# Stage edges of a fused two-layer decoder step, and the order of key groups in its sample attention

## The chip, the cores and the metric

The kernel runs on one core of a Trainium2 chip. The metric is the device time in microseconds (us), the median of three runs. One more execution was taken with the hardware profiler; all rows and line numbers come from it.

## The reference

One inference step of a hybrid trunk, here with 2 layers, for a prompt of 1024 tokens and 8 sample sequences of 8 tokens, 1088 tokens of width 1024, in fp32:

- every layer makes 6 modulation vectors per sequence from a conditioning vector (`ada = c @ w_ada + b`), modulates x with two of them, and projects it to the inputs of three head groups: gated linear attention (GLA, 4 heads), a gated linear recurrence (LRU, 256 wide) and multi-head latent attention (MLA, 8 heads, latent width 128, rotary part 32);
- the prompt tokens attend causally to themselves; each sample sequence attends to 8192 cached tokens, in a cache of pages of latent rows and rotary key rows, and to its own new tokens;
- `x <- LN(alpha * x + gate * (mix @ w_out))`, then a modulated SwiGLU feed-forward part (FFN) with hidden width 2816 and the same closing norm.

The outputs are the rows of x, the final states, and the new latent and rotary rows.

## The kernel before

`build` holds the whole program. It runs `stage_start`, and then for each layer `stage_in` (input projections, convolution, LRU), `stage_gla`, `stage_mla_prompt`, `stage_mla_sample` and `stage_out_ffn`. `run` (L200) starts a stage, and behind it clears the stage's semaphores and has all engines meet at a barrier, so nothing of a stage starts before the last instruction of the one before. Within a stage the order of the work is written out by hand, engine by engine, and semaphores tie the engines together. Loads are issued by SP (SyncE), page gathers by POOL (GpSimd).

**Three passes.** fp32 products of weights are made as three products of rounded halves: `three_passes` (L441) multiplies hi by hi (L444), then lo by hi or hi by lo (L445, L446, by operand). ACT rounds a tile to its "hi" and DVE subtracts to get the "lo"; both must be there before PE starts on the tile.

**`stage_start` (L2929).** Loads x and the first adaLN weights (WADA, 4 pieces j of 2 MB, 16 column blocks), normalizes the rows of x, and turns them back to feature-major form: 24 groups `back(g)` (L3032) of up to three 128x128 turns, kept by DVE and ACT by turns. Between them PE makes `ada(j)` (L478, 16 products each); ACT copies the rows out of PSUM (L2997). Behind all of it PE turns the 16 rows into vectors (L3045), DVE adds the bias (L450), scales (L456), and ACT (L411) and DVE (L413) modulate x into h. DVE makes the page indices there too.

**`stage_in` (L575).** Loads `w_in_B` (8 rows k), ACT rounds h and w_in_B for each k (L846, L848), DVE makes the remainders (L975), PE multiplies (first one at L444). Scans for the LRU stand at its end.

**`stage_gla` (L1061).** Works through 9 blocks of tokens in steps: `cumulate(p)` (L1122 to L1124) makes the cumulated log decay, DVE the scaled queries and keys (L1305 to L1327, the last four small products per block put the queries of each head in their own rows), `attend`, `output`. The other weights of adaLN come through here too: slabs of 1 MB (`ada_load`), for each a `pair` of products (L478, 16 of them), 24 pairs in layer 0 and 16 in layer 1, `ADA_PER_STEP` says how many in each step. POOL multiplies the LRU output by its gate at the stage's start (L1109).

**`stage_mla_prompt` (L1437).** 64 items of attention (4 pairs of heads hp, 16 items each). PE scores an item (L1597, L1599), DVE takes the negative maximum (L1775), ACT exponentiates (L1728), DVE inverts the sums, ACT scales the probabilities (L1712), PE turns them (L1609), DVE or ACT copy them (L1788), PE multiplies by the values (L1621). The head projections of the next pair (q L1569, keys L1572, latent query L1576) are put between the items: `pj_at` has ten of them at ten steps in a row, from step 5 of each 16. ACT reads them out (L1696, L1698, L1700) behind its scale of the step. POOL adds rotary parts (L1522).

**`stage_mla_sample` (L1843).** 32 pieces s, 4 for each sequence, of 2048 cached tokens. A piece has four groups of key latents and one of rotary keys (KG = 5), each of four 128x128 turns (L1910) into one of three PSUM banks, from where ACT copies three (L2002), DVE one, and ACT and DVE split the rotary group into hi (L2017) and lo (L2083). `scores` waits for all five, then makes six rotary products (L1923) and eight halves of the latent ones (L1928). Then the maximum (L2065), the exponential (L2034), `turn` (L1940), the copy of the turned probabilities (L2008, half each), `values` (L1951) and `accumulate` (L2075). PE's order for a piece is scores(s), keys(s+1) with the rotary group last, values(s-1), turn(s). Before piece 0 stands the attention to the new tokens (L1958, L1962), with a copy into the running output. Behind the last piece come a chain of small operations that joins the halves (L1976 to L2110), a product that folds them (L1985) and the value projection (L1993, DVE copies at L2116). POOL gathers the pages (L1881) and rotary rows (L1887) from the stage's start, 5 pages deep.

**`stage_out_ffn` (L2240).** SP loads w_out in 8 rows k; ACT rounds the mixed heads (L2567) and w_out (L2572), DVE makes the remainders (L2861, L2863), PE multiplies from L444. In the last layer eight products that spread the gains of the norm (L2426) stand before it. Then the FFN with its seven-product scheme, and the closing norm.

## Time and profile before

| what | us |
|---|---|
| median of 3 runs (3478.95 to 3488.6) | 3480.62 |
| profiled execution, its own time | 3485.3 |
| its span, first to last instruction | 3483.5 |
| mean granted TensorE clock, as a share of 2.4 GHz | 0.966 |
| start | 0 to 53.9 |
| layer 0: input | 53.9 to 238.2 |
| layer 0: GLA | 238.2 to 343.6 |
| layer 0: prompt attention | 343.6 to 565.9 |
| layer 0: sample attention | 565.9 to 856.1 |
| layer 0: output and FFN | 856.1 to 1766.2 |
| layer 1: input, GLA, prompt, sample, output and FFN begin at | 1766.2, 1951.4, 2049.1, 2275.3, 2565.9 |

In the rows below, PE is TensorE's matmul side and PEld its weight loads, which overlap it; DVE is VectorE, ACT ScalarE, POOL GpSimd. A line of a timeline has start, duration, engine, line of the kernel, operation, output<-inputs, and x with the count of neighbouring instructions taken together; in square brackets the idle time of the engine before it and what ended that. PEclk is the granted clock as a share of 2.4 GHz: 0.5 is the lower level, 1.2 GHz.

### The profile page before, as it was taken

How to read it: one execution, taken by the hardware profiler on the slowest of the kernel's cores; microseconds unless marked ns; L12 is line 12 of the kernel's file. 1: busy time of each engine (PE TensorE's matmuls, PEld its weight loads, DVE VectorE, ACT ScalarE, POOL GpSimd, SP SyncE). 2: the span in 40 equal slices, each digit the busy share in tenths (PEclk: the TensorE clock that was granted, in tenths of full speed). 3: DMA queues.
4: the chain of work that ended last, by engine and by line, in shares of the span. 5: the costliest groups of instructions: out<-in, count | busy, mean ns of one | idle time of the engine just before them, and what ended most of it. 6: DMA issues, size and time to landing. Idle time of an engine off the chain costs nothing. (4 is left out here: it accounts for less than half of the span.)

```text
span 3483.5 us, 61376 instructions
## 1 busy us (share of the span) xinstructions
PE 3255.1 (93%) x23676; PEld 2738.1 (79%) x23676; DVE 2326.5 (67%) x4390; ACT 1587.2 (46%) x3159; POOL 202.9 (6%) x254
## 2 busy tenths in 40 slices
PE   6988898998999999999989889989989999999997
PEld 4875566776998998999978655667769899899997
DVE  5254665444488889888844456644446888888878
ACT  5343554444255454444344445634433554544432
POOL 0020111110000000000001111011100000000000
PEclk9998999998999999999989889999989999999998
DMA  7026102443033332222121340044421333322231
GB/s 272 27 93 230 66 1 105 164 157 106 16 106 96 95 101 80 90 87 86 52 109 31 137 142 1 1 163 165 158 49 52 94 98 96 94 87 83 91 106 57
DMA packets 158149, 334.72 MB, mean 96 GB/s; under 512 B 18556, under 2 KB 85406, under 8 KB 146471
## 3 DMA queue, kind: packets, MB, share of 16 engines
q1 hardware_dynamic: 146342, 246.91, 22.2%
q0 software_dynamic: 11520, 83.89, 6.8%
q8 instruction: 193, 3.16, 0.4%
q14 instruction: 94, 0.76, 0.1%
HBM read 315.32 MB, written 15.43 MB: 95 GB/s over the span
## 5 line engine op out<-in xcount | busy, mean ns | idle before, releaser
L2494 ACT CAST w_ffn_hi<-w_ffn 128x512 fp32r<-128x512 f32 x616 | 371.3, 618 | 259.4 <-DVE w_ffn L2676 128.0
L445 PE MATMUL psum<-h_lo,w_ffn_hi 128*128 128x256 f32 (+1 forms) x1408 | 406.6, 289 | 0.0
L2688 DVE TENSOR_TENSOR w_ffn_lo<-w_ffn,w_ffn_hi 128x1024 fp32r<-128x1024 f32 (+1 forms) x366 | 383.0, 1047 | 11.8 <-ACT w_ffn_hi L2494 11.7
L444 PE MATMUL psum<-h_forms_hi,w_ffn_hi 128*128 128x288 f32 x1232 | 364.1, 296 | 3.4 <-DVE w_ffn_lo L2688 3.4
L446 PE MATMUL psum<-h_forms_hi,w_ffn_lo 128*128 128x288 f32 x1232 | 363.7, 295 | 0.0
L444 PE MATMUL psum<-h_hi,w_ffn_hi 128*128 128x256 f32 x1232 | 348.6, 283 | 10.9 <-DVE w_ffn_lo L2688 9.1
L444 PE MATMUL psum<-ffn_act_hi,w_down_hi 128*128 128x288 f32 (+1 forms) x992 | 332.3, 335 | 21.1 <-DVE w_down_lo L2694 6.5
L446 PE MATMUL psum<-h_hi,w_ffn_lo 128*128 128x256 f32 x1232 | 346.8, 281 | 0.0
L446 PE MATMUL psum<-ffn_act_hi,w_down_lo 128*128 128x288 f32 (+1 forms) x992 | 326.6, 329 | 0.0
L445 PE MATMUL psum<-ffn_act_lo,w_down_hi 128*128 128x288 f32 (+1 forms) x992 | 325.9, 328 | 0.0
L430 DVE SCALAR_TENSOR_TENSOR xT<-psum,adaT,xT 128x512 f32<-128x512 f32 (+2 forms) x320 | 191.1, 609 | 130.4 <-PE psum L446 127.0
L445 PEld LDWEIGHTS psum<-h_lo,w_ffn_hi 128*128 128x128 f32 x1408 | 265.0, 188 | 0.6
L444 PEld LDWEIGHTS psum<-h_hi,w_ffn_hi 128*128 128x128 f32 x1232 | 233.7, 190 | 15.0 <-issue 9.7
L444 PEld LDWEIGHTS psum<-h_forms_hi,w_ffn_hi 128*128 128x128 f32 x1232 | 231.3, 188 | 4.9 <-issue 2.8
L446 PEld LDWEIGHTS psum<-h_hi,w_ffn_lo 128*128 128x128 f32 x1232 | 233.9, 190 | 0.0
L446 PEld LDWEIGHTS psum<-h_forms_hi,w_ffn_lo 128*128 128x128 f32 x1232 | 231.6, 188 | 0.0
L444 PEld LDWEIGHTS psum<-ffn_act_hi,w_down_hi 128*128 128x128 f32 x992 | 186.2, 188 | 48.6 <-DVE w_down_lo L2694 15.3
L446 PEld LDWEIGHTS psum<-ffn_act_hi,w_down_lo 128*128 128x128 f32 x992 | 186.2, 188 | 14.3
L445 PEld LDWEIGHTS psum<-ffn_act_lo,w_down_hi 128*128 128x128 f32 x992 | 186.3, 188 | 12.1
L2002 ACT COPY keysT<-psum 128x512 f32<-128x512 f32 x192 | 106.8, 589 | 195.4 <-PE psum L1910 189.7
L2065 DVE TENSOR_REDUCE dec_max<-psum 128x1 f32<-128x1024 f32 x64 | 78.4, 1224 | 155.3 <-PE psum L1928 155.3
L2499 ACT CAST w_down_hi<-w_down 128x384 fp32r<-128x384 f32 (+1 forms) x240 | 116.9, 488 | 105.1 <-DMA w_down<-in_w_down 105.0
(450 smaller groups left out, 7624.8 us busy)
## 6 DMA issues: line engine op xcount, KB each, us to landing
w_ffn<-in_w_gu SPq DMA_DIRECT2D x352, 256.0 KB, 2.6
w_ada_pair<-in_w_ada SPq DMA_DIRECT2D x40, 1024.0 KB, 6.1
w_down<-in_w_down SPq DMA_DIRECT2D x192, 192.0 KB, 2.4
residual_kept<-xT SPq DMA_DIRECT2D x2, 4352.0 KB, 19.2
xT<-residual_kept SPq DMA_DIRECT2D x2, 4352.0 KB, 14.2
w_ada_first<-in_w_ada SPq DMA_DIRECT2D x4, 2048.0 KB, 22.2
w_out<-in_w_out SPq DMA_DIRECT2D x16, 512.0 KB, 7.3
w_in_T<-in_w_in_T SPq DMA_DIRECT2D x12, 512.0 KB, 4.4
```

Source lines behind the costliest of these rows:

```text
L430: ins = eng.scalar_tensor_tensor(XT[:, c, t0:t0 + wp], ps[:, 0:wp], ADA[:, gate + c, 0:1], XT[:, c, t0:t0 + wp], ALU.mult, ALU.add)
L444: pe.matmul(o, wh, xh, start=first, stop=False)
L445: pe.matmul(o, wh, xl, start=False, stop=False)
L446: return pe.matmul(o, wl, xh, start=False, stop=last)
L2002: copy(K4[:, s % 2, 4 * i:4 * i + 4].rearrange("p t k -> p (t k)"), src).then_inc(done, 1)
L2065: lk(dve.tensor_reduce(MXD[:, s % 2, :], bank(3, 2), AX.X, ALU.max))
L2494: act.copy(WGH[:, (j + 1) % NR].bitcast(F32R), WGR[:, m % 2, i]).then_inc(s_wh, 1)
L2499: act.copy(WDH[:, g % NW, 0:n].bitcast(F32R), WDR[:, g % NW, 0:n]).then_inc(s_dh, 1)
L2688: dve.tensor_tensor(WGL[:, m % 2, i:i + n].bitcast(F32R), WGR[:, m % 2, i:i + n], WGH[:, r:r + n], ALU.subtract).then_inc(s_wl, n)
```

## The change

It has these parts:

1. **Start.** The 24 backs go by token group, so that the first eight need three blocks of x. They stand ahead of `ada(j)`, and each j holds shift and scale of the same two feature tiles (WADA is loaded as eight transfers of 1 MB), so each j is turned, added and modulated by itself. Four PSUM banks for the backs instead of three. w_in_B is loaded here, behind the last back; its row k=0 and h's are split here. The page indices and a part of the constants move into layer 0's `stage_in`.
2. **Input stage.** SP fetches the first two adaLN slabs of GLA, the second behind the end of the last scan. Weights are rounded before h.
3. **GLA.** The two products of the LRU output and its gate move from POOL to DVE, behind steps 2 and 3; the first pair goes ahead of `cumulate(2)`; `ADA_PER_STEP` is shifted forward by one.
4. **Prompt attention.** Head projections are spread (`SPREAD`); from step 5 on, ACT reads them ahead of its scale. POOL gathers the first page and the first rotary rows at the end.
5. **Sample attention.** Keys of piece 0 first, new tokens beside and behind them; in each piece the rotary group is turned first and values(s-1) stand between groups two and three of the latent keys; DVE copies group three, ACT one, two and four; the sum of a piece is split from `accumulate`. At the end, the last turn stands beside the joining of the halves, the value copies are shared by DVE (even heads) and ACT (odd heads) over eight banks, four of the eight rows of w_out are fetched and k=0 is split.
6. **Output and FFN.** Only rows 4 to 7 of w_out are loaded there; buffers are laid out anew; the first rounded FFN weights wait for finer points. In the last layer the gain copy stands ahead of the roundings. w_in_B of layer 1 is loaded at the end of layer 0's FFN.

The core of the diff:

```diff
+        ADA_PER_STEP = {24: (2, 3, 3, 3, 3, 3, 3, 2, 1, 1), 16: (2, 2, 2, 2, 2, 2, 2, 1, 1, 0)}
+        MIXED_AT = (2, 3)
...
-                    for c in range(2):
-                        pool.tensor_tensor(HT[:, 2 + c], LG[:, c], XC[:, c], ALU.mult).then_inc(s_mx, 1)
...
                         todo = list(pairs_of(s - 1))
                         if s <= NBLK:
+                            for q in todo[:1] if s == 1 else ():
+                                pair(q)
                             if s + 1 < NBLK:
                                 cumulate(s + 1)
-                            for q in todo[:1]:
+                            for q in todo[:1] if s > 1 else ():
                                 pair(q)
                             attend(s - 1)
...
+                        if s in MIXED_AT:
+                            c = MIXED_AT.index(s)
+                            dve.tensor_tensor(HT[:, 2 + c], LG[:, c], XC[:, c], ALU.mult).then_inc(s_mx, 1)
...
-            for hp in range(1, HP):
-                for j in range(NPJ):
-                    pj_at.setdefault((hp - 1) * PER + 5 + j, []).append((hp, j))
+            SPREAD = {hp: (5, 8, 9, 10, 11, 12, 13, 14, 15, 16) if hp == 1 else (1, 4, 5, 8, 9, 10, 12, 13, 14, 15)
+                      for hp in range(1, HP)}
+            for hp, at_items in SPREAD.items():
+                for j, x in enumerate(at_items):
+                    pj_at.setdefault((hp - 1) * PER + x, []).append((hp, j))
...
+                    pool.wait_ge(s_pj, max(i for i, (hp, j) in enumerate(order) if proj[j][0] == "q") + 1)
+                    pool.wait_ge(s_rp, len(on_pool))
+                    pool.wait_ge(s_z, 2 + len([i for i in on_pool if proj[order[i][1]][1] == 2]))
+                    page_rows(pool, 0).then_inc(s_pf, 16)
+                    rope_rows(pool, 0).then_inc(s_pf, 16)
+                    pool.wait_ge(s_pf, 32)
...
+                        for hp, j in pj_at.get(i, []) if i > 4 else ():
+                            read(hp * NPJ + j)
                         if i:
                             scale(i - 1)
                         for blk in v_at.get(i, ()):
                             if blk % 2 == 0:
                                 v_kept(blk)
-                        for hp, j in pj_at.get(i, []):
+                        for hp, j in pj_at.get(i, []) if i <= 4 else ():
...
+                    sp.wait_ge(s_v, NS - 2)
+                    sp.wait_ge(s_s, NS - 1)
+                    for k in range(NPRE):
+                        sp.dma_start(wo(k)[0][:, 0:KD - 1], w_out_rows(k)[:, 0:KD - 1]).then_inc(s_ow[k], 16)
+                        if k == 0:
+                            sp.wait_ge(s_v, NS - 1)
+                            sp.dma_start(WOR[:, 0, KD - 1], of("w_out")[:, 0:NPRE, D - P:D]).then_inc(s_oe, 16)
+                    for k in range(NPRE):
+                        sp.wait_ge(s_ow[k], 16)
+                    sp.wait_ge(s_oe, 16)
...
                     keys(0)
-                    pe.wait_ge(s_na, 1)
+                    new_turned()
                     pe.wait_ge(s_ql, 1)
-                    for s in range(NS):
+                    for s in range(NS - 1):
                         scores(s)
-                        if s + 1 < NS:
-                            keys(s + 1)
+                        if s == 0:
+                            new_values()
+                        keys(s + 1, 0, 3)
                         if s:
                             values(s - 1)
+                        keys(s + 1, 3, KG)
+                        if s == 0:
+                            pe.wait_ge(s_na, 1)
                         turn(s)
-                    values(NS - 1)
+                    scores(NS - 1)
+                    values(NS - 2)
                     pe.wait_ge(s_mx, NS)
                     pe.transpose(bank(0)[0:SB, 0:P], NMR[:, :, NCH], ident).then_inc(s_fp, 1)
+                    turn(NS - 1)
                     pe.wait_ge(s_f, 1)
                     pe.transpose(bank(1)[:, 0:SB], HMX[:, 2, :], CST[0:SB, C_ID:C_ID + SB]).then_inc(s_fp, 1)
                     pe.wait_ge(s_f, 2)
                     pe.matmul(bank(2)[0:64, 0:SB], CST[:, C_II:C_II + 64], FND[:, 1, :], start=True, stop=True)
                     pe.matmul(bank(2)[64:P, 0:SB], CST[:, C_II:C_II + 64], FND[:, 1, :], start=True,
                               stop=True).then_inc(s_fp, 1)
+                    values(NS - 1)
...
+                    act.copy(QRH.bitcast(F32R), QRB).then_inc(s_qh, 1)
+                    rope_rounded(0)
+                    for i in A_GROUPS:
+                        key_group(act, act.copy, 0, i, s_ka)
                     act.wait_ge(s_nx, 1)
                     act.activation(SN2, SN2, ACT.Exp).then_inc(s_ne, 1)
-                    act.copy(QRH.bitcast(F32R), QRB).then_inc(s_qh, 1)
-                    for i in A_GROUPS:
-                        key_group(act, act.copy, 0, i, s_ka)
-                    rope_rounded(0)
                     for s in range(NS):
                         b, c = divmod(s, NCH)
                         if s + 1 < NS:
-                            for i in A_GROUPS[0:2]:
-                                key_group(act, act.copy, s + 1, i, s_ka)
+                            rope_rounded(s + 1)
+                            key_group(act, act.copy, s + 1, A_GROUPS[0], s_ka)
...
+                            key_group(act, act.copy, s + 1, A_GROUPS[1], s_ka)
                             key_group(act, act.copy, s + 1, A_GROUPS[2], s_ka)
-                            rope_rounded(s + 1)
+                        if s == NS - 1:
+                            act.wait_ge(s_fp, 2)
+                            act.activation(FND[:, 0, :], bank(1)[:, 0:SB], ACT.Exp).then_inc(s_fw, 1)
                         probs_turned(act, act.copy, s, 1, s_pa)
...
+                    new_start()
                     dve.wait_ge(s_qh, 1)
                     dve.tensor_tensor(QRL.bitcast(F32R), QRB, QRH, ALU.subtract).then_inc(s_ql, 1)
-                    for s in range(NS):
+                    rope_rest(0)
+                    key_group(dve, dve.tensor_copy, 0, D_GROUP, s_kd)
+                    new_probs()
+                    for s in range(NS - 1):
                         maximum(s)
-                        if s + 1 < NS:
-                            key_group(dve, dve.tensor_copy, s + 1, D_GROUP, s_kd)
-                        if s + 1 < NS:
-                            rope_rest(s + 1)
+                        if s == 0:
+                            new_kept()
+                        rope_rest(s + 1)
                         if s:
+                            sum_up(s - 1)
                             accumulate(s - 1)
+                        key_group(dve, dve.tensor_copy, s + 1, D_GROUP, s_kd)
                         probs_turned(dve, dve.tensor_copy, s, 0, s_pd)
...
+                    if not final:
+                        sp.wait_ge(s_pp, 7 * NPAIR)
+                        for k in range(KD):
+                            sp.dma_start(WBR[:, k], of("w_in_B", layer[0] + 1)[:, k]).then_inc(s_nb, 16)
+                        sp.wait_ge(s_nb, 16 * KD)
...
+            gg = [(c, n) for n in range(3) for c in range(KD)]
             STAGES = [(0, 8), (8, 16), (16, 24)]
...
+                    def rows_turned(j):
+                        pe.wait_ge(s_row, j + 1)
+                        pe.wait_ge(s_sel, 16)
+                        for x in range(4):
+                            ins = pe.matmul(bank(j)[:, x * 9:x * 9 + 9], AV1[:, j, x * P:x * P + P],
+                                            CST[:, C_SEL:C_SEL + 9], start=True, stop=True)
+                        ins.then_inc(s_done, 1)
                     for j, (g0, g1) in enumerate(STAGES):
+                        pe.wait_ge(nm, min(NBLK, 3 * j + 3))
                         for g in range(g0, g1):
                             back(g)
-                        ada(j + 1)
-                    pe.wait_ge(s_sel, 16)
-                    for j in range(NA1):
-                        pe.wait_ge(s_row, j + 1)
-                        for m in range(4 * j, 4 * j + 4):
-                            ins = pe.matmul(bank(4)[:, m * 9:m * 9 + 9], AV1[:, j, (m % 4) * P:(m % 4) * P + P],
-                                            CST[:, C_SEL:C_SEL + 9], start=True, stop=True)
-                    ins.then_inc(s_done, 1)
+                            if j and g == g0 + 3:
+                                rows_turned(j - 1)
+                        ada(j)
+                    rows_turned(2)
+                    ada(3)
+                    rows_turned(3)
...
```

## Rows read from the trace of the kernel before

**Rows 1.** Busy by stretch: us; PE, PEld, DVE, ACT, POOL; PEclk, DMA, GB/s.

```profile
238.20:343.60 105.40, 87.77 (x1033) 50.31 (x1033) 53.94 (x139) 39.14 (x113) 9.81 (x7) 0.86 0.70 246
...
565.90:856.10 290.20, 274.78 (x2430) 195.49 (x2430) 134.18 (x250) 127.11 (x259) 38.47 (x42) 0.95 0.41 146
```

**Rows 2.** PE timeline, start: start, us, operation, count [idle <-releaser].

```profile
23.48 3.60 PE L478 MATMUL psum<-w_ada_first,cT 128*9 128x512 f32 x16 [18.60 <-DMA w_ada_first<-in_w_ada]
...
38.47 3.66 PE L3032 MATMUL psum<-consts,z 128*128 128x128 f32 x24
42.06 1.90 PE L478 MATMUL psum<-w_ada_first,cT 128*9 128x512 f32 x16
43.90 3.74 PE L3045 MATMUL psum<-consts,ada_rows_first 128*128 128x9 f32 x32
57.80 0.70 PE L444 MATMUL psum<-w_in_B_hi,h_in_hi 128*128 128x432 f32 x1 [10.16 <-DVE w_in_B_lo L975]
```

**Rows 3.** ACT timeline, end of the start stage.

```profile
48.40 4.63 ACT L411 ACTIVATE hT<-xT,adaT 128x1024 f32<-128x1024 f32 x4 [3.78 <-DVE adaT L456]
```

**Rows 4.** The page's DMA issues: KB each, median us to landing.

```profile
w_ada_pair<-in_w_ada SPq DMA_DIRECT2D x40, 1024.0 KB, 6.1
```

**Rows 5.** DVE timeline in GLA, layer 0.

```profile
241.17 5.56 DVE L1327 TENSOR_TENSOR gla_q_blocks<-gqT,gla_exps 32x128 f32<-32x128 f32 x4
...
247.83 1.17 DVE L1327 TENSOR_TENSOR gla_q_blocks<-gqT,gla_exps 32x128 f32<-32x128 f32 x4
```

**Rows 6.** POOL timeline in GLA, layer 0.

```profile
241.33 4.95 POOL L1109 TENSOR_TENSOR hT<-lgateT,lru_xc 128x1088 f32<-128x1088 f32 x2
```

**Rows 7.** PE timeline in GLA, layer 0.

```profile
246.78 1.22 PE L1122 MATMUL psum<-consts,log_forget 128*128 128x256 f32 x2 [6.76 <-DVE gla_q_blocks L1327]
...
248.57 1.74 PE L478 MATMUL psum<-w_ada_pair,cT 128*9 128x256 f32 x16
```

**Rows 8.** Waits, prompt attention, layer 0: us in total, times, longest.

```profile
PE psum L1572 <- ACT kT L1698: 6.4, 3, 2.1
...
PE psum L1569 <- ACT qT L1696: 2.4, 3, 0.8
...
PE psum L1576 <- ACT q_latT L1700: 1.5, 3, 0.5
PE psum L1609 <- ACT probs_long L1712: 1.5, 3, 0.5
```

**Rows 9.** PE timeline, start of the sample attention, layer 0.

```profile
568.97 1.06 PE L1958 MATMUL psum<-consts,scores_new_shifted 64*64 64x64 f32 x8 [4.97 <-ACT scores_new_shifted L2019]
570.80 3.67 PE L1962 MATMUL psum<-ckv_sample,probs_newT 64*64 64x128 f32 x16 [0.78 <-DVE probs_newT L2057]
574.40 3.55 PE L1910 MATMUL psum<-consts,pages 128*128 128x128 f32 x16
...
581.02 0.74 PE L1923 MATMUL psum<-keys_krT_hi,q_rope_hi 64*128 64x512 f32 x2 [2.63 <-DVE q_rope_lo L2088]
...
590.37 0.49 PE L1923 MATMUL psum<-keys_krT_hi,q_rope_hi 64*128 64x512 f32 x2 [0.79 <-DVE keys_krT_lo L2083]
```

**Rows 10.** PE timeline, one steady piece of the sample attention.

```profile
703.58 0.49 PE L1923 MATMUL psum<-keys_krT_hi,q_rope_hi 64*128 64x512 f32 x2
...
706.34 1.99 PE L1910 MATMUL psum<-consts,pages 128*128 128x128 f32 x16
...
711.67 0.49 PE L1923 MATMUL psum<-keys_krT_hi,q_rope_hi 64*128 64x512 f32 x2
```

**Rows 11.** ACT timeline in the same piece.

```profile
709.28 0.59 ACT L2002 COPY keysT<-psum 128x512 f32<-128x512 f32 x1
```

**Rows 12.** PE timeline, first output product of layers 0 and 1.

```profile
862.75 0.76 PE L444 MATMUL psum<-mix_hi,w_out_hi 128*128 128x512 f32 x1 [8.04 <-DVE w_out_lo L2863]
...
2577.59 0.48 PE L444 MATMUL psum<-mix_hi,w_out_hi 128*128 128x512 f32 x1 [4.25 <-DVE w_out_lo L2863]
```

**Rows 13.** PE timeline, first product of layer 1.

```profile
1770.13 0.70 PE L444 MATMUL psum<-w_in_B_hi,h_in_hi 128*128 128x432 f32 x1 [8.81 <-DVE w_in_B_lo L975]
```

470 lines of the change are left out of this document (286 added, 184 removed).

## The prediction

> **What bounds the kernel now.** I read the stretches stage by stage first, to see where TensorE is not the bound. In the sample attention PE is busy 274.78 of 290.20 us; GLA is the loose one, 87.77 of 105.40 at a granted clock of 0.86 in layer 0 [rows 1], and layer 1 has the same pattern. The FFN's arithmetic is untouched. So the change can earn only where PE stands still or runs at 1.2 GHz for want of work, and that is at the stage edges, in GLA and in the prompt attention's short waits. I then read PE's timeline at each of these places, the other engines' rows beside it for what it waits on, and one steady piece of the sample attention, which occurs 32 times per layer, to see what reordering it can cost.
>
> All sums are against the profiled execution, 3485.3 us (span 3483.5, 1.8 around it). It lies 4.7 above the median of the three runs, 3480.62; I take that off at the end.
>
> **Start.** Now: the last 16 adaLN products end near 43.9, then 32 turns of 3.74 for all vectors at once, then DVE and ACT modulate, a barrier, a load and a rounding; PE's next matmul is at 57.80 after 10.16 idle [rows 2]. New order on PE: eight backs, ada(0), eight backs, turn(0), ada(1), eight backs, turn(1), ada(2), turn(2), ada(3), turn(3). The backs are the same 24 per third (3.66 us), an ada is 1.90, one turn a quarter of 3.74, 0.94 [rows 2]. The first third needs only three blocks of x and can lie in the 18.60 of idle before ada(0), which starts at 23.48 when its weights land [rows 2]; I let it overhang to 24.3, since the smaller loads stand behind x in the same queue. ada(0) then ends at 26.2 (at 1.90, not the 3.60 it takes now from a cold engine), two rounds of 3.66 + 0.94 + 1.90 = 6.5 at 39.2, turn(2) at 40.1, ada(3) at 42.0, its copy and turn about 44, with 1.0 of handovers 45. Behind it stand the last quarter's vectors and one modulate piece each (4.63/4 = 1.16 on ACT [rows 3]), two sample operations and one weight remainder, near 47.2; the barrier 1.2; the first matmul of the input projection at about 48, since w_in_B is in SBUF and its k=0 is split. Gain 57.8 - 48 = **10** (9 to 12). The w_in_B load waits for the last back, near 37, so it has 10 us; the first 1 MB slab of the GLA weights takes 6.1 to land [rows 4] and this load is 1.8 MB, so it can be the last thing in: that is the lower end. The page indices (24 tiny DVE operations) go behind the scans, under the last input products: nothing, or at most their 4 us once, were that cover gone. The constants' remainder and its cast go into the input stage, behind the first loads: nothing.
>
> **End of the input stage, both layers.** Two 1 MB slabs are now fetched before GLA. SP issues the second after the second lru output is final, about 5 us ahead of the stage's end, and one takes 6.1 in the median, with others in flight [rows 4]. 0.3 per layer (0 to 1): **-0.6**.
>
> **GLA.** VectorE's four small products for the masked queries take 5.56 us for token block 0 and 1.17 for block 1 [rows 5]. In the first case GpSimd multiplies gate by lru output in that very time, 4.95 us from 241.33 [rows 6], and PE waits 6.76 for DVE [rows 7]. The change takes both products off POOL and puts them on DVE in steps 2 and 3, 1.3 us each, where DVE has 3 and 8 us of slack. That removes 5.56 - 1.17 = 4.4. It also puts the first pair of adaLN products (1.74 [rows 7]) into the gap that is left. In layer 0 one more pair then lies ahead of the last attend (23 for 22), which gives that 1.7 back; layer 1 has 16 both times. 4.4 + 6.1 = **10.5**. Bounds: 4 (only the first if DVE is then late in steps 2, 3) to 16, since both stretches run partly at 1.2 GHz and a denser start may keep 2.4.
>
> **Prompt attention.** Three waits, each three times per layer: 6.4 for kT, 2.4 for qT, 1.5 for q_latT, 10.3 together [rows 8]. All are head projections that PE issues before ACT has read the earlier one out, because ACT's read sits behind its scale. The change spaces these items over more steps and puts the read ahead of the scale. A projection waits for its bank when two follow each other; spaced by one step of about 3 us they do not, except the first two of some heads. 8.5 of 10.3, both layers: **17**. Bounds 8 to 20: ACT scales a step later, which PE's turns could notice; at the lower end half of the waits come back as waits for the scaled probabilities. POOL's first page and rope rows are gathered behind its last rope add, at about step 45 of 64, and land under the rest: nothing.
>
> **Sample attention, start.** Now its first scores come at 581.02, 15.1 after the stage's 565.9, and the second at 590.37 [rows 9]. From the first key turn to the first scores is 581.02 - 574.40 = 6.6; the eight small turns are 1.06 [rows 9]. With the page in SBUF the keys start with the stage: 0.2 + 6.6 + 1.1 = 7.9 to the first scores. The new values (3.67) go behind them. That moves them off the front but keeps them ahead of scores(1), with more key copies to follow, so that not all of the 7.2 is kept: scores(1) at 19 instead of 24.5. Gain 5.5 per layer, **11** (8 to 17). These turns are slow now: 3.55 for sixteen [rows 9], 1.99 in the steady piece [rows 10], that is 1.2 against 2.4 GHz, behind a stretch in which PE mostly idled; I took them at the slow value. The Trainium skill (TensorE: Matmul & The Clock Gate, Part 4: PE-mode transpose) says that transposes don't count as PE-busy for the clock. By that rule opening the stage with 28 turns would hold scores(0) and the new values at 1.2 GHz longer, some 2 to 3 us per layer, and the sum would be 5 lower; in the trace the scores after the turns are slow too (0.74 for two against 0.49), but behind an idle of 2.63, so it does not decide.
>
> **Sample attention, steady.** One piece lasts 711.67 - 703.58 = 8.08, PE without a gap [rows 10]. The new order has the same instructions and the same changes of kind: no gain. What moves is the last copy before the scores. Take the end of the scores (706.34) as 0: rope turned at 0.6, groups one and two at 1.6, values to 3.5, groups three and four to 4.6, turn to 5.3 (scores at 711.67 - 706.34 = 5.33). ACT copies the fourth group in 0.59 [rows 11]: ready at 5.15 and a handover of 0.1, against 5.33. On the DVE side the rope remainder now follows the maximum directly and the third group is copied by 4.8. So the slack falls to about 0.1. Cost: 0 to 0.2 for 62 pieces, 0 to 12; the order fits by my sum, so **-2**.
>
> **Sample end and output edge.** Layer 0: PE's first output product is at 862.75 behind 8.04 of idle, 6.6 behind the stage's start [rows 12]. Half of w_out (4 of 8 rows) and the k=0 split now lie before the barrier, under the tail: the first product comes right at the start, -6.5; the tail itself (last turn beside the chain of maxima, value copies shared with ACT) ends 5 earlier; of both 11.3. Layer 1: the eight ones-products and their copy stay ahead: first product at 2577.59 [rows 12] becomes about 2570.6: 7.0. Together **18.3** (14 to 21). Cover: the other rows are issued at the stage's start and needed 22 us later.
>
> **FFN and layer 1's input.** Buffers are laid anew, and waits of the first rounded weights come at finer points: nothing. w_in_B is fetched behind layer 0's last product, under the closing norm. The first matmul, at 1770.13 [rows 13], 3.9 behind the stage's start at 1766.2, no longer waits for the load, but still for the roundings of weight and h and their remainders, some 3.1: **0.8** (0 to 1).
>
> Sum: 10 - 0.6 + 10.5 + 17 + 11 - 2 + 18.3 + 0.8 = **65**. 3485.3 - 65 = 3420.3; less 4.7, **3416**.
>
> **Rivals.**
> (a) Moved gaps. ACT or DVE bounds the prompt attention and PE waits for scaled probabilities in place of kT; the turns hold the clock low as in the rule above; the w_in_B and w_out loads end last at the edges. Prompt 8, sample start 6, edges 20, GLA 6, steady -4: 36, giving 3445. For: each is a lower bound above. Against: in the prompt attention each of the three waits names ACT's read; those for scaled probabilities are 1.5 in all [rows 8].
> (b) Slower: the steady piece loses its cover. The place is ACT: the fourth key copy ends behind the turn, then the probability copy behind that, so that the next exp is late as well. If ACT needed 1.05 us more than PE's 8.08 in each piece, 62 x 1.05 = 65 eats everything; at 1.3 it is 3480.6 + 16 = 3497. For: the slack is only 0.1. Against: ACT is busy 127.11 us in 32 pieces, under 4.0 of each 8.08 [rows 1], so a late copy costs its lateness and does not pile up.
> (c) The change does not do what it says at the steady piece but is merely late by the 0.2: -12, total 55, 3426. It lies inside the range.
> (d) GLA and the prompt attention earn more than I allow, since the clock stays up where gaps close: 1.2 GHz stretches in GLA are worth some 6 more per layer at most; 3400.
>
> **Numbers.** Forecast (with c and d inside) 0.76; (a) 0.18; nearly no change, by a stall of 0.9 to 1.1 per piece, 0.03; (b) 0.03. 0.3% of this kernel, 10.4 us, is about what a measurement can tell from nothing; (a) still gains three times that. Faster 0.94, same 0.03, slower 0.03. Range: 3397 to 3442: below is 1 in 10 that most terms reach their upper bounds, above is 1 in 10, half of (a) and (b).
>
> **What would show it.** PE's first input product near 48; the wait at the first forgetting-gate product of GLA down from 6.76 to about 2 or filled by a pair; no kT row over 1 us among the waits; first scores 8 us behind the sample stage's start, and whether they run 0.74 or 0.49; a piece still 8.1 long; first output product at the stage's edge. A piece of 8.3 or more, or waits for the scaled probabilities of several us, would prove me wrong.

## Result, and the profile after

The changed kernel takes 3388.45 us (median of 4 runs, 3385.45 to 3389.21), the kernel before 3479.78 beside it; the ratio is 0.9732, with a 95% interval of 0.9713 to 0.9751. It is faster, as forecast, but by 91 us, where 65 were forecast and 3397 was the lower end of the range. TensorE's mean granted clock was 0.976 to 0.978 in these four executions; over 32 executions of the kernel before, beside the runs below, it was 0.964 to 0.969, and their times lay between 3471.91 and 3483.78.

The totals of the page (busy time of each engine, share of the span, instructions), first before, then after:

```profile
PE 3255.1 (93%) x23676; PEld 2738.1 (79%) x23676; DVE 2326.5 (67%) x4390; ACT 1587.2 (46%) x3159; POOL 202.9 (6%) x254
```

```profile
PE 3223.4 (95%) x23676; PEld 2720.9 (80%) x23676; DVE 2324.1 (69%) x4405; ACT 1591.2 (47%) x3166; POOL 194.2 (6%) x250
```

The span went from 3483.5 to 3386.7, 96.8 less. TensorE has the same 23676 matmuls, yet is busy for 31.7 us less. Its idle time, span less busy, is 228.4 before and 163.3 after: 65.1 less. So the gain has two parts, and they have to be read apart: **gaps that were closed (65) and the same matmuls at a higher granted clock (32)**. The sum of the prediction was 65 and is, but for one adaLN group taken at full clock, a sum of gaps. The two parts are not independent: experiment 3 shows a wait of 2.44 for VectorE that is gone, and with it idle time, where the products around it ran at half clock.

The same by stage, from the stretches between the stages' first instructions (length and PE busy; idle is their difference; "half" is the time at 1.2 GHz, summed from the trace's clock records, which begin 27 to 28 us behind the start, and up to the end of the last computation):

| stage | length before, after | idle before, after | busy before, after | half before, after |
|---|---|---|---|---|
| start | 54.0, 53.5 | 28.8, 24.9 | 25.2, 28.7 | 5, 9 |
| input 0 | 184.3, 179.3 | 5.4, 2.1 | 178.8, 177.2 | 12, 4 |
| GLA 0 | 105.4, 98.3 | 17.7, 10.1 | 87.8, 88.2 | 29, 28 |
| prompt 0 | 222.3, 214.5 | 18.5, 10.9 | 203.8, 203.7 | 11, 10 |
| sample 0 | 290.3, 275.8 | 15.5, 7.8 | 274.8, 268.0 | 27, 14 |
| output, FFN 0 | 910.1, 902.2 | 35.9, 28.6 | 874.2, 873.6 | 26, 17 |
| input 1 | 185.1, 182.4 | 5.8, 5.4 | 179.4, 177.0 | 13, 7 |
| GLA 1 | 97.7, 77.4 | 16.0, 9.4 | 81.7, 68.1 | 45, 11 |
| prompt 1 | 226.5, 211.6 | 20.3, 9.8 | 206.2, 201.8 | 15, 7 |
| sample 1 | 290.4, 274.7 | 15.4, 7.5 | 275.0, 267.2 | 28, 10 |
| output, FFN 1 | 917.6, 917.1 | 49.2, 47.0 | 868.4, 870.0 | 26, 27 |

Three of these stretches as the view gives them, for layer 0's sample attention and layer 1's GLA after, and for the latter before (columns as in [rows 1]); the first answers to the second of [rows 1]:

```profile
545.61:821.39 275.78, 267.98 (x2430) 192.19 (x2431) 135.72 (x249) 132.64 (x266) 37.15 (x40) 0.98 0.44 153
...
1905.92:1983.36 77.44, 68.05 (x873) 40.87 (x873) 51.86 (x140) 36.05 (x105) 4.90 (x5) 0.93 0.56 199
```

```profile
1951.35:2049.06 97.71, 81.70 (x873) 47.45 (x873) 53.70 (x138) 36.23 (x105) 9.81 (x8) 0.77 0.52 179
```

Layer 1's GLA is the largest single gain, 20.3 us, and two thirds of it is the clock: 0.77 before, 0.93 after, for the same 873 matmuls.

**Start**, PE's timeline after, against [rows 2]:

```profile
22.60 2.82 PE L3200 MATMUL psum<-consts,z 128*128 128x128 f32 x12 [5.43 <-DVE xT L3258]
25.35 2.74 PE L477 MATMUL psum<-w_ada_first,cT 128*9 128x512 f32 x16
...
39.92 3.60 PE L477 MATMUL psum<-w_ada_first,cT 128*9 128x512 f32 x16
44.23 1.06 PE L3207 MATMUL psum<-consts,ada_rows_first 128*128 128x9 f32 x8 [0.71 <-ACT ada_rows_first L3155]
45.22 1.90 PE L477 MATMUL psum<-w_ada_first,cT 128*9 128x512 f32 x16
49.10 1.06 PE L3207 MATMUL psum<-consts,ada_rows_first 128*128 128x9 f32 x8 [1.98 <-ACT ada_rows_first L3155]
53.56 0.70 PE L443 MATMUL psum<-w_in_B_hi,h_in_hi 128*128 128x432 f32 x1 [3.40 <-PEq L198]
```

The first input product is at 53.56, not at 48. The first third of the backs ends at 25.35, one us late, because PE waits 5.43 for DVE to empty the banks. The clock is at half from 37.3 to 44.1, so ada(2) takes 3.60 for 1.90. Then the turn of the last group's rows waits 1.98, since ACT's copy stands behind a rounding and a modulation. w_in_B was in at 47.9 and never late.

**GLA**, PE's timeline after, against [rows 7]:

```profile
234.53 1.05 PE L477 MATMUL psum<-w_ada_pair,cT 128*9 128x256 f32 x16
236.98 0.70 PE L1142 MATMUL psum<-consts,log_forget 128*128 128x256 f32 x2 [1.40 <-DVE gla_q_blocks L1349]
```

The wait of 6.76 is 1.40, with the pair in front of it.

**Prompt attention**, waits of PE in layer 0 after, against [rows 8]:

```profile
PE psum L1606 <- DMA w_uq<-in_mla_w_uq: 3.1, 1, 3.1
PE psum L1668 <- ACT v L1750: 2.1, 1, 2.1
PE psum L1579 <- PEq L198: 1.3, 1, 1.3
PE psum L1643 <- ACT probs_long L1746: 1.1, 3, 0.5
```

The waits for kT, qT and q_latT are gone, and nothing came for the probabilities (1.1 where 1.5 was). What came in layer 0 is a wait of 3.1 for the load of w_uq, which lands 9.9 us behind the stage's start and landed after 7.5 before. In layer 1 that wait is 1.7, and it was there before, with 2.3:

```profile
PE psum L1572 <- DMA w_uq<-in_mla_w_uq: 2.3, 1, 2.3
```

**Sample attention**, its start, and a steady piece, against [rows 9, 10]:

```profile
545.64 0.85 PE L1984 MATMUL psum<-consts,pages_kr 128*128 128x128 f32 x4 [1.65 <-PEq L198]
...
553.01 0.79 PE L1997 MATMUL psum<-keys_krT_hi,q_rope_hi 64*128 64x512 f32 x1
...
557.33 1.96 PE L2039 MATMUL psum<-ckv_sample,probs_newT 64*64 64x128 f32 x16
...
563.41 0.50 PE L1997 MATMUL psum<-keys_krT_hi,q_rope_hi 64*128 64x512 f32 x2
...
707.75 0.50 PE L1997 MATMUL psum<-keys_krT_hi,q_rope_hi 64*128 64x512 f32 x2
...
715.77 0.50 PE L1997 MATMUL psum<-keys_krT_hi,q_rope_hi 64*128 64x512 f32 x2
```

ACT's copy of the last key group in that piece, against [rows 11]:

```profile
706.99 0.59 ACT L2088 COPY keysT<-psum 128x512 f32<-128x512 f32 x1 [0.96 <-PE psum L1984]
```

The first scores are 7.4 behind the stage's start (7.9 forecast), the second ones 17.8 (19). The new values take 1.96, where they took 3.67 in front of everything. A piece lasts 8.02.

The start of layer 1's sample attention, after, differs in its clock, which is at half until 2198.0 and again from 2201.4 to 2204.8:

```profile
2194.99 1.08 PE L1984 MATMUL psum<-consts,pages_kr 128*128 128x128 f32 x4 [1.95 <-PEq L198]
2195.87 1.91 PE L1984 MATMUL psum<-consts,pages 128*128 128x128 f32 x8
2198.65 1.10 PE L1984 MATMUL psum<-consts,pages 128*128 128x128 f32 x8 [0.87 <-DVE keys_krT_lo L2185]
```

**Output edge**, first products of layers 0 and 1, against [rows 12]:

```profile
821.41 0.47 PE L443 MATMUL psum<-mix_hi,w_out_hi 128*128 128x512 f32 x1 [2.25 <-PEq L198]
...
2480.54 0.50 PE L443 MATMUL psum<-mix_hi,w_out_hi 128*128 128x512 f32 x1 [1.96 <-ACT gain_rows L2708]
```

From the last scores to the output stage it is 17.4 (803.99 to 821.39) where it was 23.2 (832.97 to 856.14).

### The profile page after: what moved, and what is told of

Same layout as the page of the kernel before. It is cut to its first block and busy times, and to the rows that moved or that the text cites. A ratio compares the mean times of both kernels' runs of the same rounds, so it can differ in the third digit from the quotient of the medians.

```text
span 3386.7 us, 61424 instructions
## 1 busy us (share of the span) xinstructions
PE 3223.4 (95%) x23676; PEld 2720.9 (80%) x23676; DVE 2324.1 (69%) x4405; ACT 1591.2 (47%) x3166; POOL 194.2 (6%) x250
## 5 line engine op out<-in xcount | busy, mean ns | idle before, releaser
L444 PE MATMUL psum<-h_forms_lo,w_ffn_hi 128*128 128x288 f32 x528 | 155.5, 295 | 0.0
## 6 DMA issues: line engine op xcount, KB each, us to landing
w_ada_first<-in_w_ada SPq DMA_DIRECT2D x8, 1024.0 KB, 18.5
```

Source lines behind the costliest of these rows:

```text
L444: pe.matmul(o, wh, xl, start=False, stop=False)
```

## Experiments

Where a table of stages is spoken of, it is the one above, made for the kernel in question.

**1. GLA undone in the changed kernel.**

```diff
-        MIXED_AT = (2, 3)
...
+                    for c in range(2):
+                        pool.tensor_tensor(HT[:, 2 + c], LG[:, c], XC[:, c], ALU.mult).then_inc(s_mx, 1)
...
-                            for q in todo[:1] if s == 1 else ():
-                                pair(q)
```

> The changed kernel with GLA as before: both products on GpSimd, first pair behind the third cumulate, old numbers of pairs per step. Theory A (the clock follows the closed wait in the stage itself): the wait of 6.8 us is back in both layers and the half-clock stretches of layer 1's GLA with it; that stage goes from 77.4 back to 95 or more, PE busy in it from 68 to about 80, and the total is 22 to 30 us above the changed kernel, near 3414. Theory B (the clock there follows from what other parts of the change do, as the preloaded slabs): only idle time comes back, 4 to 7 us per layer, PE busy stays near 68, total near 3399.

3407.31 us (4 runs, 3402.17 to 3410.01), ratio to the kernel before 0.9795 (0.9779 to 0.9812). PE's wait is back, with VectorE's four products as long as before:

```profile
240.86 1.22 PE L1143 MATMUL psum<-consts,log_forget 128*128 128x256 f32 x2 [6.76 <-DVE gla_q_blocks L1348]
```

```profile
235.25 5.55 DVE L1348 TENSOR_TENSOR gla_q_blocks<-gqT,gla_exps 32x128 f32<-32x128 f32 x4
```

The two GLA stages are 110.7 and 92.8 us long, 12.4 and 15.3 more: idle 4.0 and 5.5, busy 8.5 and 9.9. In all it is 19 us above the changed kernel, between the two theories: in the profiled execution the two GLA stages are 28 longer and all the others together 7 shorter. The clock does come back down with the gaps, but not as layer 1's stage alone had it.

**2. GLA alone in the kernel before.** The edit is the reverse of the first, without the slabs fetched early.

> The kernel before with the GLA part of the change alone (both products on VectorE, first pair ahead, pairs shifted; no slab is preloaded). Theory A: layer 0's GLA near 98, layer 1's near 78, half-clock time in layer 1's GLA from about 50 to about 14 us, total 25 to 30 below the kernel before, near 3452. Theory B: 10 to 11 us less in all, near 3469, with layer 1's PE busy still near 81.

3466.31 us (10 runs, 3460.39 to 3481.12) beside 3476.91, ratio 0.9977 (0.9962 to 0.9992): the smaller figure, 10 us or less. Idle fell by 3.9 in each stage and not by 7. The trace says why:

```profile
241.24 1.86 PE L478 MATMUL psum<-w_ada_pair,cT 128*9 128x256 f32 x16 [4.40 <-DMA w_ada_pair<-in_w_ada]
```

The pair that should fill the gap waits 4.40 for its slab. So the reordering can't pay without the fetch in the input stage, which I had costed as 0.6 lost.

**3. The two products moved alone, in the kernel before.**

```diff
-                        pool.tensor_tensor(HT[:, 2 + c], LG[:, c], XC[:, c], ALU.mult).then_inc(s_mx, 1)
...
+                        if s in (2, 3):
+                            c = (2, 3).index(s)
+                            dve.tensor_tensor(HT[:, 2 + c], LG[:, c], XC[:, c], ALU.mult).then_inc(s_mx, 1)
```

> The kernel before with one edit: the two products of LRU output and gate are on VectorE in GLA's steps 2 and 3 instead of on GpSimd. Theory A (VectorE's four small products were held up by GpSimd reading SBUF): they take 1.2 us instead of 5.6, PE's wait before the third cumulate goes from 6.8 to about 2.4, idle falls by 4.4 in each of the two stages, 8.8 in all. Rival (the wait only moves to VectorE's steps 2 and 3, or to the slabs): idle falls by less than 3 per layer. The clock comes on top of it, in either direction.

```profile
239.18 0.70 PE L1120 MATMUL psum<-consts,log_forget 128*128 128x256 f32 x2 [2.37 <-DVE gla_q_blocks L1325]
```

```profile
237.96 1.17 DVE L1325 TENSOR_TENSOR gla_q_blocks<-gqT,gla_exps 32x128 f32<-32x128 f32 x4
```

1.17 where 5.56 was, and the wait 2.37 where 6.76 was: 4.4, as forecast. The total is 3468.9 in one run. In idle time layer 0's GLA gained 8.0 and layer 1's 3.8. The 8.0 overstates what the edit does. PE's wait for DVE near the end of layer 0's GLA is in the kernel before, but not here, where the same turns ran at half clock (first before, then this run):

```profile
340.60 0.99 PE L1186 MATMUL psum<-consts,gla_o 128*128 128x128 f32 x4 [2.44 <-DVE gla_o L1382]
```

```profile
337.75 4.44 PE L1184 MATMUL psum<-consts,gla_o 128*128 128x128 f32 x18
```

The move alone thus saves about as much idle time per stage as experiment 2 did with all the GLA edits, and the further 3 that the changed kernel has need the fetched slabs. No run has the slabs and the move without the reordering, so what the reordering itself adds is not shown.

Layer 1's stage went to 81.7 us with 12 us at half clock, while layer 0's went to 108.5 with 51 (29 before): the same edit met the clock in opposite ways in the two layers. PE busy over the whole kernel was 3250.6 here and 3245.6 in experiment 2, both inside the range of the old work (experiment 5): these edits alone bring no gain in clock to the kernel before.

**4. The prompt attention undone in the changed kernel.**

```diff
-            SPREAD = {hp: (5, 8, 9, 10, 11, 12, 13, 14, 15, 16) if hp == 1 else (1, 4, 5, 8, 9, 10, 12, 13, 14, 15)
+            SPREAD = {hp: tuple(range(5, 5 + NPJ))
...
-                        for hp, j in pj_at.get(i, []) if i > 4 else ():
+                        for hp, j in ():
```

> The changed kernel with the prompt attention's head projections at ten steps in a row again and ACT's read behind its scale. By the prediction's step the three waits of 10.3 us per layer come back: the prompt stages go from 214.5 and 211.6 to about 222 to 224 and 219 to 222, total 16 to 20 above the changed kernel, near 3406. The rival (the gain in these stages came from the stages before, over the clock and the edges): less than 8 in all.

3426.42 us in one run, 38 above the changed kernel. The three waits are back to the tenth:

```profile
PE psum L1606 <- ACT kT L1732: 6.4, 3, 2.1
PE psum L1606 <- DMA w_uq<-in_mla_w_uq: 3.8, 1, 3.8
PE psum L1603 <- ACT qT L1730: 2.4, 3, 0.8
...
PE psum L1610 <- ACT q_latT L1734: 1.5, 3, 0.5
```

Idle rose by 10.6 and 8.7 in the two stages, 19.3 for a forecast of 17. The other half of the 38 is PE's busy time, and much of it in a stage whose code is not touched: layer 1's GLA is 88.9 us long instead of 77.4, with idle 9.2 as in the changed kernel and 36 us at half clock for 11.

**5. Other placements of the same work.** A few writes of VectorE to PSUM at the end of the start stage shift all that follows; three kernels with the changed work and two with the work of before.

```diff
+                    for _x in range(3):
+                        dve.memset(bank(_x), 0.0)
```

> The changed kernel with three extra writes on VectorE (about 1.8 us in all) at the end of the start stage, so everything behind it is shifted against the start of the program. Theory A (the clock follows the work of each stage): the total grows by 1.8 us, near 3390, and every later stage has its length within 1 us. Theory C (where the half-clock stretches fall is a matter of how the work lies against the moments at which the clock is set): some stages change by 3 to 15 us, in either direction, most likely the two GLA stages.

> The changed kernel with one extra write on VectorE (0.6 us) at the end of the start stage. Theory C: idle time grows by 0.6, the sum of half-clock time falls anywhere between 125 and 165 us and the total between 3378 and 3394; the sample stages keep 7 to 17 us of half-clock time each, against 27 in the kernel before. A theory by which the changed kernel's clock is fixed by its work alone has every stage within 1 us of the changed kernel.

> The changed kernel with four extra writes (about 2.4 us) at the end of the start stage. Half-clock time between 125 and 165 us, PE busy between 3215 and 3228, total 3380 to 3396. A value above 190 would say that the changed kernel's clock is luck of placement.

> The kernel before with three extra writes on VectorE (about 1.8 us) at the end of the start stage. Theory C (the place of the half-clock stretches moves with such a shift): idle grows by 1.8 us only, but single stages change by 3 us or more and the total by up to 8 in either direction; the total of half-clock time stays above 200 us, far from the 143 and 130 us of the changed kernel without and with a delay. If it falls to 150 here, the changed kernel's gain in clock was luck of placement and not of its closed gaps.

> The kernel before with one extra write (0.6 us) at the end of the start stage: another placement of the same work. Half-clock time between 205 and 245 us, PE busy between 3245 and 3260, total 3472 to 3486. A value under 180 would say that placement alone can give what the change gave.

| kernel | writes | us | span | idle | PE busy | half clock |
|---|---|---|---|---|---|---|
| changed | 0 | 3388.48 | 3386.7 | 163 | 3223.4 | 143 |
| changed | 1 | 3383.37 | 3381.5 | 163 | 3218.9 | 137 |
| changed | 3 | 3384.75 | 3382.7 | 166 | 3216.5 | 130 |
| changed | 4 | 3381.28 | 3379.1 | 165 | 3213.8 | 126 |
| before | 0 | 3485.3 | 3483.5 | 228 | 3255.1 | 236 |
| before | 1 | 3473.58 | 3471.8 | 227 | 3244.4 | 218 |
| before | 3 | 3480.87 | 3479.1 | 230 | 3249.1 | 221 |

Each row is one profiled execution. No delayed kernel is slower, and single stages move a good deal: with three writes layer 0's GLA is 91.9 us long instead of 98.3 and layer 1's 79.3 instead of 77.4; with one write they are 94.1 and 83.7. So the work of a stage doesn't fix its clock. That the writes did it is not shown, since each row stands for one execution and the kernel before, unchanged, moved by 12 us over 32 of them. But the two groups don't touch: busy 3213.8 to 3223.4 against 3244.4 to 3255.1, a difference of 31 between their means (3218.2 and 3249.5). **So the clock's gain belongs to the change, with some 5 us either way from one execution or placement to the next.** The sample stages are the steadiest in this: 21 to 31 us at half clock in the three kernels with the work of before, 5 to 14 in the four with the changed work.

**6. GLA and prompt attention both undone.** The edits of 1 and 4 together.

> The changed kernel with both GLA and the prompt attention as before, so that the edges and the sample attention alone are changed. If the idle times of the parts add up, idle is 159 + 9 + 19 = 187 or so, against 224 in the kernel before. If the clock's gain is a matter of many closed gaps, half-clock time is near that of the kernel before, 190 to 225 us, less 15 in each sample stage; if it is luck of placement it is anywhere from 130. Total near 3440.

3441.97 us in one run. Idle is 194 (span less busy), or 190 without the 4 us of stores behind the last computation, which the expectation's 159 and 187 leave out: the gaps add up. PE is busy 3245.8 with 201 us at half clock, near the kernel before. With one of the two undone it was 3235.1 (GLA) and 3241.9 (prompt), with neither 3218.2 on average. By these numbers the clock's gain does not add up over the parts: undoing GLA gives back 17 of it, the prompt attention 24, both together 28 and not 41. Each of the three is one execution, though, with the 5 us either way of experiment 5, and the two kernels of experiment 10, which open no gap, lie 6 and 9 above the mean too (3224.2 and 3226.7).

**7. Values behind all the keys again.**

```diff
-                        keys(s + 1, 0, 3)
+                        keys(s + 1)
                         if s:
                             values(s - 1)
-                        keys(s + 1, 3, KG)
...
+                        key_group(dve, dve.tensor_copy, s + 1, D_GROUP, s_kd)
+                        if s:
                             accumulate(s - 1)
-                        key_group(dve, dve.tensor_copy, s + 1, D_GROUP, s_kd)
```

DVE's key copy goes ahead of `accumulate` with it.

> The changed kernel with the values of the last piece behind all five key groups again (the rope group still first; VectorE copies its key group ahead of the accumulation). My prediction had the changed order cost up to 0.2 us per piece; the trace shows 8.02 for a piece where the kernel before has 8.08. If the place of the values makes the difference, a piece is 8.08 or more here and the sample stages grow by 2 to 5 us each; if the rope group at the front makes it, they stay at 275 to 276 and the total within 2 us of the changed kernel, apart from where the half-clock stretches fall.

3443.06 us (4 runs), ratio 0.9897 (0.9879 to 0.9915): 55 slower than the changed kernel. The place of the values makes the difference, but at 25 us per sample stage where I gave 2 to 5. A piece takes 8.91 (704.57 to 713.48 between first scores), and in each there is this:

```profile
709.54 1.09 PE L1984 MATMUL psum<-consts,pages 128*128 128x128 f32 x8 [0.67 <-DVE keys_krT_lo L2184]
```

The fourth of the five groups needs the bank of the rope group, which DVE gives back only when it has taken the maximum (1.22) and the remainder (0.69). With the values in between, that time is PE's work. The rope group at the front and the values in the middle are one change: the first alone costs 0.8 us a piece against the kernel before.

**8. First page gathered in the sample stage again.**

```diff
-                    page_rows(pool, 0).then_inc(s_pf, 16)
-                    rope_rows(pool, 0).then_inc(s_pf, 16)
...
+                    rope_rows(pool, 0).then_inc(s_p0, 16)
+                    page_rows(pool, 0).then_inc(s_p0, 16)
                     for s in range(1, NS):
```

> The changed kernel with the first page and the first rotary rows gathered at the start of the sample stage again, as the first two of its queue. If the fetched page is what lets the first keys stand at the stage's start, PE waits for the gather, 8 us or so: the first scores slip from 7.7 to about 15 us behind the stage's start and each sample stage grows by 6 to 8, 12 to 16 in all, near 3402. If the order of keys and new tokens alone made the gain, the stages grow by less than 3.

3415.76 us in one run, 27 above. PE stands for 12.45 us at the start, the barrier included:

```profile
558.68 1.12 PE L1987 MATMUL psum<-consts,pages_kr 128*128 128x128 f32 x4 [12.45 <-DMA pages<-in_cache_ckv,piece_row]
```

Idle rises by 9.7 and 9.1 in the two sample stages, while PE is busy 2.0 and 1.3 less in them, so that they are 7.7 and 7.8 longer. The rest of the 27 lies elsewhere: the two GLA stages, whose code is not touched, are 3.5 and 11.5 longer with 10 and 25 us more at half clock, and all the others together 3 shorter. From one execution it can't be told whether the edit moved that clock or whether it would have moved anyway.

**9. w_out loaded in the output stage again.** The four rows' loads and the split of k=0 go back.

```diff
-            s_ow = [sem(f"w_out_{k}_in") for k in range(NPRE, KD)]
+            s_ow = [sem(f"w_out_{k}_in") for k in range(KD)]
...
-                    for k in range(1, KD):
+                    for k in range(KD):
```

> The changed kernel with all rows of w_out loaded, and k=0 split, in the output stage again. By the prediction's step the first output product of layer 0 goes from the stage's edge back to 6.6 us behind it, that of layer 1 from 10.9 to about 12 to 13 us behind; the sample stages end some 0.5 us sooner. Idle grows by 6 in layer 0 and by 1 to 2 in layer 1, total 7 to 9 above the changed kernel. Rival (the gain at this edge lies in the tail of the sample stage and not in the fetched rows): less than 3.

3396.14 us in one run, 7.7 above the changed kernel.

```profile
822.09 0.77 PE L443 MATMUL psum<-mix_hi,w_out_hi 128*128 128x512 f32 x1 [8.08 <-DVE w_out_lo L2978]
```

This is 6.7 behind the stage's start, as it was. Sample stage and output stage together are 7.2 longer in layer 0 and 3.6 in layer 1, more than I gave layer 1, whose first product is 13.1 behind its stage's start and was 10.9. The other stages together are 3 shorter. The other part of the edge, the tail, stays gained.

**10. Two orders and three.** An attempt to do better.

```diff
                     sp.dma_start(WUK1, of("mla_w_uk")[:, 4 * NOPE:8 * NOPE]).then_inc(s_inw, 16)
-                    sp.dma_start(WUV, of("mla_w_uv")).then_inc(s_inv, 16)
                     sp.dma_start(WUQ, of("mla_w_uq")).then_inc(s_inq, 16)
+                    sp.dma_start(WUV, of("mla_w_uv")).then_inc(s_inv, 16)
+                    sp.wait_ge(s_inq, 16)
...
                             act.copy(HIN[:, 0].bitcast(F32R), HT[:, 0]).then_inc(s_h0, 1)
+                            kept_row(NA1 - 1)
```

> The changed kernel with two edits of order. In the prompt attention w_uq is loaded ahead of w_uv, and SP issues the stores only when it is in: PE's wait for it, 3.1 us in layer 0 and 1.7 in layer 1, should go (4 us in all). In the start stage ACT copies the last adaLN rows ahead of the modulation of the third pair of tiles: PE's last wait, 1.98, falls to under 1 and the stage ends 1 us earlier. Total 5 below the changed kernel, near 3383; half-clock placement may hide it, the idle time of the stages must show it. Rival: the stores, held back, or VectorE, as the bound of the start, take it back: less than 2 us of idle in all.

3386.26 us (5 runs, 3374.37 to 3392.02), ratio 0.9728 (0.9709 to 0.9747). The wait for w_uq is gone from both layers (idle 2.4 and 1.0 less in the prompt stages), and the start stage ends at 51.9 instead of 53.5. In the total nothing can be told from the changed kernel: half-clock time was 157 in the profiled run.

The third order puts the third adaLN group ahead of the last eight backs:

```diff
-                        ada(j)
-                    rows_turned(2)
-                    ada(3)
+                        ada((0, 1, 3)[j])
+                        if j == 1:
+                            ada(2)
```

> The kernel with the two orders changed (w_uq first, last adaLN rows copied early) and one more in the start stage: the third group of adaLN products stands ahead of the last eight backs and its rows are copied and turned among them. PE then has less to do behind the last back: the start stage ends 1.5 to 2.5 us earlier than with the two orders alone (51.9 to about 50), bound by VectorE's modulation. Rival: those products wait for their weights, which land near 34, and the backs behind them slip by as much: no gain or a loss of 1 us. Total near 3383, with the placement of the half-clock stretches deciding what a comparison can see.

3384.72 us (5 runs), ratio 0.9726 (0.9713 to 0.9739), no difference either, and the start stage ends at 53.8, later and not earlier. The rival was wrong as well: the weights were there.

```profile
31.55 3.92 PE L477 MATMUL psum<-w_ada_first,cT 128*9 128x512 f32 x32
...
42.58 3.60 PE L477 MATMUL psum<-w_ada_first,cT 128*9 128x512 f32 x16
48.54 1.87 PE L3211 MATMUL psum<-consts,ada_rows_first 128*128 128x9 f32 x8 [2.35 <-ACT ada_rows_first L3156]
```

What lost is the clock, at half from 40.7 for 17.1 us: the last group took 3.60, the last turn 1.87, and ACT's copy stood in its queue.

## Why the prediction was right and wrong

**Right in kind.** Most mechanisms did what they were said to do: no stall at the steady piece, no wait for the probabilities, no preload that ended a stage late. And the idle time fell by the forecast sum:

| term | forecast | idle time saved | busy time saved |
|---|---|---|---|
| start and input 0 (with slab) | 9.7 | 7.3 | -1.9 |
| input 1 (with slab) | 0.5 | 0.4 | 2.4 |
| GLA | 10.5 | 14.2 | 13.2 |
| prompt attention | 17 | 18.1 | 4.5 |
| sample attention, output edge | 27.3 | 25.1 | 13.5 |
| sum | 65 | 65.1 | 31.7 |

That the sum of idle time meets 65 to the tenth is luck: its terms miss by -2.4, -0.1, +3.7, +1.1 and -2.2, and idle time itself moves with the clock.

**The step that failed** is the one at the head of the working: the change can earn "only where PE stands still or runs at 1.2 GHz for want of work", after which each term was priced by gaps alone. As a saving, the clock stood in the sum only with one adaLN group (1.90 for 3.60), and beside it in one bound of one term (GLA up to 16) and in rival (d), with "some 6 more per layer at most" and 3400. So the sum put a term at nothing that measured 31, as the difference of PE's busy time over four placements of the changed work and three of the old; layer 1's GLA gave 13.7 of it in the profiled run. The rows hinted at it: [rows 1] gave a granted clock of 0.86 for a stage whose gaps I was closing, and [rows 9] a start at half clock. A term for the clock had to stand in the sum.

**Start, too large by 6.** "Gain 57.8 - 48" was 4.2 (57.80 to 53.56). Against my chain, ada(1) ends 0.8 late (33.5 for 32.7), since DVE is late with the banks of the first backs; from there ada(2) ends after 10.0 and not 6.5, at half clock from 37.3; and the last turn ends 0.8 later still, as ACT's copy of the rows queues behind what the change itself put there. I had costed handovers at PE, and not read ACT's queue or the clock.

**Preloaded slabs, wrong sign.** Costed as -0.6, they are what GLA's gain beyond the 4.4 per stage needs: without them all its edits save 3.9 of idle time per stage, with them 7.6 and 6.6.

**GLA's gap, right in its wait** (4.4 from VectorE's products, experiment 3), **too small in the rest:** 10.5 forecast, 14.2 of idle time measured. How the further gain is shared between slabs and pair is open, and it holds some idle time that moves with the clock.

**Prompt attention, right:** 19.3 by undoing for 17. The wait for w_uq, 3.1 in layer 0 where none was and 1.7 in layer 1 where 2.3 was, was missed. "Half of the waits come back" did not occur.

**Sample start, right:** 7.4 and 17.8 for 7.9 and 19; but the price of not having the page is 9.1 to 9.7 us per layer, which no step named. In layer 1 the first scores are 6.3 behind the stage's start and the second 16.8. The rule that I weighed there can be read now, and the traces speak on both sides. In layer 0 the granted clock was at half for the turns of keys(0) and the first scores (0.79 for one), and rose at 556.1, 3.1 us behind the first scores; the new values ran at full, 1.96. In the start stage it fell at 37.3, in the midst of gapless turns with only eight small products among them, and stayed at half through ada(2). The Trainium skill (TensorE: Matmul & The Clock Gate, Part 4: PE-mode transpose) has transposes not counting as PE-busy for the clock: the start stage agrees with that. Layer 1's sample stage does not: there the clock rose at 2198.0, when PE had made nothing in the stage but the first twelve turns, and the next eight took 1.10, at full. With one write more at the start (experiment 5) layer 0 did the same. So the rule is not borne out as it stands. The 2 to 3 us per layer that it would have cost were not lost; before, the same turns and values had run at half as well.

**Steady piece, wrong sign of a small term.** -2 forecast, about +4 measured (8.02 for 8.08, 62 pieces). ACT's last key copy ends at 706.99 + 0.59 = 707.58, the scores start at 707.75: slack 0.17, where I had 0.1. Rival (b) had the right place for danger and the wrong engine. The order breaks at DVE and the rope group's bank (experiment 7), and for that the values' place is the cover.

**Edge, right in layer 0** (6.6 for the first product and 5.8 for the tail: 12.4 for 11.3) **and in layer 1** (0.8 and 5.8: 6.6 for 7.0). Of rival (a) only the low clock under the turns came true, in the start stage and at layer 0's sample start.

What stays open: why half-clock stretches fall in one stage and not in another. In experiments 4 and 8 a stage of unchanged code, layer 1's GLA, is 11.5 us longer, and in experiment 3 one edit moves the two GLA stages in opposite directions. No run here foretells which.

## What to carry to other kernels

Price a closed gap twice: the wait itself, and the work around it that ran at 1.2 GHz. The second was twice the first in layer 1's GLA (granted clock 0.77 before) and nothing in layer 0's (0.86), so it belongs in the range as much as in the sum. Judge an edit by its own waits in the trace, since a stage's idle time also falls where its clock is low, and judge the clock by several executions and placements of the same work: layer 1's GLA was 77.4 to 83.7 us long over four of them. And undo the parts one at a time before calling one free: the fetched slabs and the place of the values looked like costs and were what made their neighbours pay.

## What was not expected of the hardware

With extra VectorE writes at the start the changed kernel was no slower (3388.5 without, 3381.3 to 3384.8 with one, three or four, one run each). VectorE's four 32x128 products took 5.55 to 5.56 us beside a GpSimd product on SBUF and 1.17 without, in every kernel. TensorE's clock rose from half to full 3.0 us into layer 1's sample stage, behind twelve 128x128 turns and no other product since the stage began. The same load of w_uq, in the same place of its queue, landed between 7.0 and 9.9 us behind its stage's start over the two layers of the fifteen profiled executions that have this order. A wait of 2.44 for VectorE in the kernel before was gone in experiment 3, where the same turns ran at half clock.
